# Weight chunks with seven block products: another order of sums, splits and settlements, and other places for the last chunk's slabs

## The chip, the cores and the metric

The kernel runs on one core of one Trainium2 chip. The metric is the device time in microseconds (us); three runs of the kernel before gave 1120.53, 1124.59 and 1125.94 us, median 1124.59.

## The reference, cut to what matters

Two decoder layers over 512 prompt tokens and 32 sample tokens (544 columns): a recurrent mixer in layer 0, windowed attention in layer 1, and behind each mixer the same MLP, which is what the change touches.

```python
D_MODEL = 1024
D_FF = 4 * D_MODEL

def squared_relu_mlp(x, w_up, w_down):
    return jnp.square(jax.nn.relu(x @ w_up)) @ w_down
...
        xp = layer_norm(ALPHA * xp + squared_relu_mlp(xp, mlp_w_up[i], mlp_w_down[i]), ln2_g[i], ln2_b[i])
```

All products are float32 in quality. The kernel splits each operand into a rounded high part and the rest, and multiplies high by high, high by rest and rest by high: three matmuls for one.

## The kernel before

The hidden width of 4096 is cut into 8 chunks of 512. Tokens are taken in two halves, of 256 and 288 columns. Chunk 0 and chunk 7 of a layer are computed plainly. Chunks 1 to 6 use seven block products for eight, both for the up product (x times w_up) and for the down product (hidden times w_down). Each chunk has an up half of seven products, which TensorE does in the order U11, UT1, UT2, U21, UT3, UT4, U22, and a down half, D11, DT1, DT2, D22, DT3, D21, DT4. Each product is 24 matmuls, of 256 columns in U11, U21, U22, D11, D22 and D21 and of 288 in the others, with two waits for banks, one ahead of each half of it. Chunks 2 to 5 are one rolled loop (Fori), so one order of instructions serves all of them.

The names without a T are blocks of the weights as they lie in memory. The names with a T are sums of blocks, and the DMA makes them: a block stands in one of four stage buffers, and POOL issues a DMA that adds another block onto it (L2055). So stage buffers are chains: U11 becomes UT1, then UT2, then UT4, and then the next chunk's U11 is loaded there. U22 becomes UT3, then D22 is loaded and becomes DT3. U21 and D21 take turns in the third. D11 becomes DT1, then DT2, then DT4 in the fourth. In chunk 1 alone, UT2 and UT4 stand in a buffer of their own, first_raw. A link of a chain can start only when the split of the one before it is done.

Splitting one weight (split_in) is an ACT copy that rounds into w_hi (L808) and a DVE subtraction into w_lo (L1315). TensorE waits for the second. ACT must also wait until the place in w_hi that it writes has been used up (PLACE, BEFORE, slot_free).

What ACT does between splits: keep (L1041) copies a finished up product from a bank so that the next product can add onto the bank. Product j has two tiles t, so keep(2, 0) takes the first tile of UT2, keep(4, 0) the first tile of UT3. UT2's tile t waits for keep(0, t), UT3's for keep(2, t), UT4's for keep(4, t). rectify, square_hi, square_raw and part_hi make from the kept sums the seven inputs of the down half, H11, H22, H12 and their sums S1 to S4. DVE adds banks onto kept products (combine, L1696), makes sums (part_sum, L1708) and the rest parts (part_lo, L1704), and settles each pair of down banks into acc (settle, L1719). In the order of the down products: D11 reads H11, DT1 S1, DT2 S2, D22 S4, DT3 S3, D21 H12, DT4 H22.

Every engine runs its own list in the order in which the code is written. So an instruction that waits holds up all that stands behind it on its engine, and the order by hand in chunk (one for each engine), load_around (SP, plain loads, L673) and all_sums (POOL, adding loads) is what the change rewrites. The tables ROUND_WEIGHT, REST_WEIGHT, SETTLE_ORDER, KEEP_ORDER and REST_ORDER repeat those orders so that waits get the right counts.

Chunk 7's four up slabs were ordinary jobs: load on SP behind all of chunk 6's loads, split by L802 on ACT and L1309 on DVE. group_by_half is TensorE's loop over them. In layer 0, POOL then issues the loads and copies of the attention caches (L2108 to L2112).

## Time and profile before

| | |
|---|---|
| median of three runs | 1124.59 us |
| profiled execution | 1123.91 us, of which the span of the program is 1121.7 us |
| TensorE busy | 1067.0 us, 95% |
| VectorE (DVE) busy | 845.0 us, 75% |
| ScalarE (ACT) busy | 665.9 us, 59% |
| GpSimd (POOL) busy | 226.4 us, 20% |
| mean granted TensorE clock | 0.97 of full |

The layer-0 MLP chunks 1 to 7 run from 220 to 530 us of the span, those of layer 1 from 770 to 1095 us. A chunk is about 43 to 52 us. Times in rows are from the start of the span. A row of the timeline gives the start, the duration, engine, line and operation, and in brackets how long the engine sat idle before it and who ended that.

### The profile page before, as it was taken

Reading aid. Unit: us, or ns where it says so; the run is one execution under the profiler, and the core shown is the slowest. Engines: PE = TensorE matmul, PEld = TensorE weight load, DVE = VectorE, ACT = ScalarE, POOL = GpSimd, SP = SyncE. Lnnn points to the kernel's source line nnn. Section 1 sums busy time; section 2 is a strip of 40 time slices with the busy share of each in tenths; the row PEclk is TensorE's granted clock in tenths of the full one; section 3 lists DMA queues with packets and bytes.
Section 4 is the critical chain, followed back from the end, with each engine's and each line's share of the span. In section 5 each row is a group of like instructions: output and inputs, shape, how many; then the busy total and the mean of one; then the engine's idle time right before and its main releaser. Section 6 shows DMA issues by size and latency. Waiting matters only on the chain.

```text
span 1121.7 us, 21627 instructions
## 1 busy us (share of the span) xinstructions
PE 1067.0 (95%) x8247; PEld 1040.7 (93%) x8247; DVE 845.0 (75%) x1289; ACT 665.9 (59%) x1159; POOL 226.4 (20%) x285
## 2 busy tenths in 40 slices
PE   8999999989999999899999999998999999998996
PEld 8999999989999899899999778998999899898995
DVE  6999898868778777586875664896868678585775
ACT  5999857554654636453667775665654636445343
POOL 1111042011111111111244463200111111111023
PEclk9999999989999999998999999999999999998998
DMA  7322406176787686773141220262787686866502
GB/s 241 114 86 94 132 18 190 39 151 141 163 200 150 137 180 137 184 203 123 28 124 44 76 58 20 76 151 59 167 189 150 134 183 151 175 143 132 150 1 80
DMA packets 54460, 139.54 MB, mean 124 GB/s; under 512 B 5632, under 2 KB 21440, under 8 KB 54368
## 3 DMA queue, kind: packets, MB, share of 16 engines
q0 software_dynamic: 14512, 53.60, 27.4%
q1 hardware_dynamic: 39584, 84.32, 22.8%
q8 instruction: 50, 0.82, 0.3%
q10 hardware_dynamic: 288, 0.59, 0.2%
q14 instruction: 26, 0.21, 0.1%
HBM read 135.95 MB, written 3.56 MB: 124 GB/s over the span
## 4 chain that ended last, share of the span: by engine, by line
PE 57%; DMA 17%; DVE 12%; issue 6%; ACT 6%; POOL 2%; DVEq 0%; SPq 0%; ACTq 0%; POOLq 0%
DMA stage<-w_up 10%; PE bank L2167 8%; PE bank L2168 7%; PE bank L2169 7%; DMA stage<-w_down 7%; DVE w_lo L1315 5%; PE bank L2422 3%; PE bank L2424 3%; PE bank L2423 3%; PE bank L2254 3%; PE bank L2443 3%; PE bank L2441 3%; PE bank L2442 3%; PE bank L2255 3%; PE bank L2256 3%
## 5 line engine op out<-in xcount | busy, mean ns | idle before, releaser
L808 ACT ACTIVATE w_hi<-stage 128x1024 fp32r<-128x1024 f32 x164 | 170.5, 1055 | 246.7 <-DMA stage<-w_up 117.1
L1315 DVE TENSOR_TENSOR w_lo<-stage,w_hi 128x1024 fp32r<-128x1024 f32 x164 | 194.8, 1219 | 78.0 <-ACT w_hi L808 77.8
L2441 PE MATMUL bank<-part_hi,w_hi 128*128 128x288 f32 (+1 forms) x672 | 194.9, 290 | 0.4 <-DVE part_lo L1704 0.3
L2443 PE MATMUL bank<-part_hi,w_lo 128*128 128x288 f32 (+1 forms) x672 | 194.8, 290 | 0.0
L2442 PE MATMUL bank<-part_lo,w_hi 128*128 128x288 f32 (+1 forms) x672 | 194.4, 289 | 0.0
L2167 PE MATMUL bank<-x_hi,w_hi 128*128 128x288 f32 (+1 forms) x496 | 145.2, 293 | 1.0 <-issue 1.0
L2168 PE MATMUL bank<-x_lo,w_hi 128*128 128x288 f32 (+1 forms) x496 | 143.7, 290 | 0.0
L2169 PE MATMUL bank<-x_hi,w_lo 128*128 128x288 f32 (+1 forms) x496 | 143.1, 288 | 0.0
L2441 PEld LDWEIGHTS bank<-part_hi,w_hi 128*128 128x128 f32 x672 | 127.2, 189 | 0.8 <-issue 0.5
L2442 PEld LDWEIGHTS bank<-part_lo,w_hi 128*128 128x128 f32 x672 | 127.5, 190 | 0.0
L2443 PEld LDWEIGHTS bank<-part_hi,w_lo 128*128 128x128 f32 x672 | 127.3, 189 | 0.0
L2422 PE MATMUL bank<-s_hi,w_hi 128*128 128x288 f32 (+1 forms) x384 | 114.5, 298 | 9.4 <-ACT h L1041 9.3
L1719 DVE TENSOR_TENSOR acc<-acc,bank 128x512 f32<-128x512 f32 (+1 forms) x168 | 113.0, 709 | 8.9 <-PE bank L2443 8.8
L2423 PE MATMUL bank<-s_lo,w_hi 128*128 128x288 f32 (+1 forms) x384 | 112.9, 294 | 0.0
L2424 PE MATMUL bank<-s_hi,w_lo 128*128 128x288 f32 (+1 forms) x384 | 112.7, 294 | 0.0
L2422 PE MATMUL bank<-x_hi,w_hi 128*128 128x256 f32 (+1 forms) x288 | 89.5, 311 | 22.8 <-ACT h L1041 19.0
L2055 POOL DMA_DIRECT2D stage<-w_down x48 | 41.4, 863 | 267.7 <-DVE w_lo L1315 267.7
L2167 PEld LDWEIGHTS bank<-x_hi,w_hi 128*128 128x128 f32 x496 | 93.2, 188 | 2.3 <-issue 2.1
L2169 PEld LDWEIGHTS bank<-x_hi,w_lo 128*128 128x128 f32 x496 | 93.4, 188 | 0.0
L2168 PEld LDWEIGHTS bank<-x_lo,w_hi 128*128 128x128 f32 x496 | 93.3, 188 | 0.0
L2055 POOL DMA_DIRECT2D stage<-w_up x44 | 41.7, 949 | 253.5 <-DVE w_lo L1315 231.6
L2254 PE MATMUL bank<-x_hi,w_hi 128*128 128x256 f32 (+1 forms) x288 | 85.0, 295 | 5.3 <-DVE acc L1719 5.3
(293 smaller groups left out, 2954.8 us busy)
## 6 DMA issues: line engine op xcount, KB each, us to landing
stage<-w_up SPq DMA_DIRECT2D x54, 512.0 KB, 3.9
stage<-w_down SPq DMA_DIRECT2D x52, 512.0 KB, 5.8
stage<-w_down POOLq DMA_DIRECT2D x48, 512.0 KB, 5.5
stage<-w_up POOLq DMA_DIRECT2D x44, 512.0 KB, 7.4
stage<-w_qkv SPq DMA_DIRECT2D x10, 512.0 KB, 4.3
stage<-w_x SPq DMA_DIRECT2D x8, 512.0 KB, 5.0
stage<-w_y SPq DMA_DIRECT2D x8, 512.0 KB, 3.4
stage<-w_out SPq DMA_DIRECT2D x8, 512.0 KB, 3.7
```

What stands on the lines that cost most here:

```text
L808: A(w_hi[:, slot_of(l, k), :], raw_of(l, c, k), ACT.Copy).then_inc(s_whi, 1)
L1315: vt.tensor_tensor(w_lo[:, s, :], raw_of(l, c, k), w_hi[:, s, :].bitcast(F32), ALU.subtract)\
L2167: mm(out, wh, xh, start=(k == 0), stop=False)
L2168: mm(out, wh, xl, start=False, stop=False)
L2169: ins = mm(out, wl, xh, start=False, stop=(k == last))
L2254: mm(out, wh, xh, start=(k == 0), stop=False)
L2422: mm(out, wh, xh[:, k, :], start=(fresh and k == 0), stop=False, skip_group_check=True)
L2423: mm(out, wh, xl[:, k, :], start=False, stop=False, skip_group_check=True)
L2424: ins = mm(out, wl, xh[:, k, :], start=False, stop=(k == 3), skip_group_check=True)
L2441: mm(out, wh, xh[:, k, :], start=(fresh and k == 0), stop=False, skip_group_check=True)
L2442: mm(out, wh, xl[:, k, :], start=False, stop=False, skip_group_check=True)
L2443: ins = mm(out, wl, xh[:, k, :], start=False, stop=(k == 1), skip_group_check=True)
```

## The change

The arithmetic stays the same: every product, split, sum and settlement of before is there once. What changes is the order and some places.

- POOL: the sum UT1 of the next chunk is issued ahead of DT4 instead of behind it, and UT2 and UT3 of the next chunk follow at the end of a chunk's list in place of the start of the next one's.
- SP: the next chunk's D11 is loaded at the end of a chunk's list, ahead of U21.
- ACT and DVE: another order of splits, keeps, squares, rest parts and settlements in a chunk. On ACT, D22's split now stands ahead of keep(4, 0), and square_hi and square_raw of H11 behind it; the splits DT3, D21 and the next UT1 stand ahead of part_hi of S4. On DVE, DT2's split stands ahead of the sum S2, and the next UT1's split ahead of D21's.
- Places in w_hi and w_lo are dealt out anew, so that the waits of slot_free follow.
- First chunk: U22 is split straight behind UT1, and UT2 behind the first accumulation, both ahead of the down sums of chunk 0; on ACT ahead of the second scaling of the residual.
- Last chunk: its four up slabs are loaded and split inside chunk 6, where the next chunk's U11, UT1, U22 and UT2 would be (bring_slab, slab_in).
- POOL's cache loads in layer 0 wait until the last down slab of chunk 7 is split.

The diff, cut to its core:

```diff
@@ -78,29 +78,30 @@
 H11, H22, S1, S2, H12, S4, S3, H21 = range(8)
 HIDDEN_WIDTH = {H11: 256, H12: 256, S4: 256, H22: HW, S1: HW, S2: HW, S3: HW}
 ROUND_ORDER = (H11, H22, S1, H12, S3, S2, S4)
-REST_ORDER = (H11, H22, S1, S2, H12, S4, S3)
+REST_ORDER = (H11, H22, S1, H12, S2, S4, S3)
...
-
-
-FIRST = (U11, UT1, UT2, U22)
-ROUND_WEIGHT = ((D11, 0), (U21, 0), (UT3, 0), (UT4, 0), (DT1, 0), (D22, 0), (U11, 1), (DT2, 0), (D21, 0), (DT3, 0),
-                (DT4, 0), (UT1, 1), (U22, 1), (UT2, 1))
-REST_WEIGHT = ((D11, 0), (U21, 0), (UT3, 0), (UT4, 0), (DT1, 0), (D22, 0), (U11, 1), (DT2, 0), (DT3, 0), (D21, 0),
-               (UT1, 1), (DT4, 0), (U22, 1), (UT2, 1))
+PLACE = {U11: 0, UT3: 0, UT1: 1, U22: 2, DT2: 2, UT2: 3, UT4: 3, DT3: 3, U21: 4, D22: 4,
+         D11: 5, D21: 5, DT1: 6, DT4: 6}
+BEFORE = {U11: (UT3, -1), UT3: (U11, 0), UT1: (UT1, -1), U22: (DT2, -1), DT2: (U22, 0), UT2: (DT3, -1), UT4: (UT2, 0),
+          DT3: (UT4, 0), U21: (D22, -1), D22: (U21, 0), D11: (D21, -1), D21: (D11, 0), DT1: (DT4, -1), DT4: (DT1, 0)}
+
+
+FIRST = (U11, UT1, U22, UT2)
+ROUND_WEIGHT = ((D11, 0), (U21, 0), (UT3, 0), (UT4, 0), (DT1, 0), (D22, 0), (U11, 1), (DT2, 0), (DT3, 0), (D21, 0),
+                (UT1, 1), (DT4, 0), (U22, 1), (UT2, 1))
+REST_WEIGHT = ((D11, 0), (U21, 0), (UT3, 0), (UT4, 0), (DT1, 0), (D22, 0), (U11, 1), (DT2, 0), (DT3, 0), (UT1, 1),
+               (D21, 0), (DT4, 0), (U22, 1), (UT2, 1))
 SPLITS = len(ROUND_WEIGHT)
-KEEP_ORDER = ((0, 0), (0, 1), (2, 1), (2, 0), (4, 0), (4, 1), (5, 1))
+SLAB_AFTER = (U11, UT1, U22, UT2)
+KEEP_ORDER = ((0, 0), (0, 1), (2, 0), (2, 1), (4, 0), (4, 1), (5, 1))
 COMBINE_ORDER = (U21, UT1, U22)
 RECTIFY_ORDER = (H11, H22, H12)
 SQUARE_ORDER = (H11, H22, H21, H12)
-SETTLE_ORDER = ((0, 0), (0, 1), (1, 0), (2, 0), (1, 1), (2, 1), (3, 0), (3, 1), (4, 0), (4, 1), (5, 0), (6, 0),
-                (6, 1), (5, 1))
+SETTLE_ORDER = ((0, 0), (0, 1), (1, 1), (1, 0), (2, 0), (2, 1), (3, 0), (3, 1), (4, 0), (4, 1), (5, 1), (5, 0),
+                (6, 0), (6, 1))
 SUM_ORDER = (S1, S3, S2, S4)
 
...
+            for n in (0, 0, 0, 1):
+                loads[(st0 + n) % STAGES] += 16
+                up_slab_at[l].append(((st0 + n) % STAGES, loads[(st0 + n) % STAGES]))
...
@@ -675,16 +688,29 @@
             def load_around(l, c, i=0):
 
                 last = c == CHUNKS - 2
-                if c > 1:
-                    bring(l, c, D11, s_xd, down_block(l, c, 0, 0, i), split_done(l, c - 1, DT4, i))
                 bring(l, c, D22, s_yin, down_block(l, c, 1, 1, i), split_done(l, c, UT3, i))
                 if not last:
                     bring(l, c + 1, U11, s_xu, up_block(l, c + 1, 0, 0, i), split_done(l, c, UT1 if c == 1 else UT4, i))
+                else:
+                    bring_slab(l, 0)
                 bring(l, c, D21, s_zin, down_block(l, c, 1, 0, i), split_done(l, c, U21, i))
                 if not last:
                     bring(l, c + 1, U22, s_yin, up_block(l, c + 1, 1, 1, i), split_done(l, c, DT3, i))
+                else:
+                    bring_slab(l, 1)
+                    bring_slab(l, 3)
+                    bring_slab(l, 2)
+                if not last:
+                    bring(l, c + 1, D11, s_xd, down_block(l, c + 1, 0, 0, i), split_done(l, c, DT4, i))
                 if not last:
                     bring(l, c + 1, U21, s_zin, up_block(l, c + 1, 1, 0, i), split_done(l, c, D21, i))
+
+            def bring_slab(l, k):
+
+                c = CHUNKS - 2
+                sp.wait_ge(*(split_done(l, c, UT4), split_done(l, c + 1, 0), split_done(l, c + 1, 1), split_done(l, c, DT3))[k])
+                st = up_slab_at[l][k][0]
+                sp.dma_start(stage[:, st, :], up_quad(l, c + 1, k)).then_inc(s_arrived[st], 16)
 
...
-                for k in range(4):
-                    load(j7 + k, up_quad(l, CHUNKS - 1, k))
...
+
+            def slab_in(l, k):
+
+                st, count = up_slab_at[l][k]
+                w = job_at[("chunk", l, CHUNKS - 1)][1] + k
+                act.wait_ge(s_arrived[st], count)
+                act.wait_ge(*free_at[w - SLOTS])
+                A(w_hi[:, w % SLOTS, :], stage[:, st, :], ACT.Copy).then_inc(s_whi, 1)
...
@@ -1069,51 +1101,59 @@
 
                 first, last = c == 1, c == CHUNKS - 2
                 h_low, h_mid, h_far = h11[:, :, 0:256], h12[:, :, :], h22[:, :, :]
+                keep(l, c, i, 0, 0, 4, h11[:, 0, 0:256])
                 split_in(l, c, D11, i)
-                keep(l, c, i, 0, 0, 4, h11[:, 0, 0:256])
                 split_in(l, c, U21, i)
+                if first:
+                    token_sum(l, 4, s4_hi[:, :, :], raw_b[:, :, 0:256])
                 split_in(l, c, UT3, i)
                 keep(l, c, i, 0, 1, 4, h11[:, 1, 0:256])
                 if first:
-                    token_sum(l, 4, s4_hi[:, :, :], raw_b[:, :, 0:256])
-                split_in(l, c, UT4, i)
-                keep(l, c, i, 2, 1, 4, h12[:, 1, :], -1.0)
-                if first:
                     act.wait_ge(s_slo, 4 * l + 3)
                     token_sum(l, 3, s3_hi[:, :, :], raw_a[:, :, :])
+                split_in(l, c, UT4, i)
                 keep(l, c, i, 2, 0, 4, h12[:, 0, :], -1.0)
+                keep(l, c, i, 2, 1, 4, h12[:, 1, :], -1.0)
                 split_in(l, c, DT1, i)
                 rectify(l, c, i, H11, h_low)
+                split_in(l, c, D22, i)
+                keep(l, c, i, 4, 0, 4, h22[:, 0, :], -1.0)
                 square_hi(l, H11, h_low)
-                square_raw(h_low)
-                keep(l, c, i, 4, 0, 4, h22[:, 0, :], -1.0)
-                split_in(l, c, D22, i)
                 keep(l, c, i, 4, 1, 4, h22[:, 1, :], -1.0)
                 if not last:
                     split_in(l, c + 1, U11, i)
+                else:
+                    slab_in(l, 0)
                 rectify(l, c, i, H22, h_far)
+                square_raw(h_low)
                 square_hi(l, H22, h_far)
                 keep_rectified(l, c, i)
                 square_raw(h_far)
                 act.wait_ge(*kept(l, c, 5, 1, i))
                 square_raw(h21[:, :, :])
+                part_hi(l, c, i, S1)
                 split_in(l, c, DT2, i)
-                part_hi(l, c, i, S1)
                 rectify(l, c, i, H12, h_mid)
                 square_hi(l, H12, h_mid)
                 part_hi(l, c, i, S3)
                 square_raw(h_mid)
                 part_hi(l, c, i, S2)
+                split_in(l, c, DT3, i)
                 split_in(l, c, D21, i)
+                if not last:
+                    split_in(l, c + 1, UT1, i)
+                else:
+                    slab_in(l, 1)
                 part_hi(l, c, i, S4)
-                split_in(l, c, DT3, i)
                 split_in(l, c, DT4, i)
                 if not last:
-                    split_in(l, c + 1, UT1, i)
-                if not last:
                     split_in(l, c + 1, U22, i)
+                else:
+                    slab_in(l, 2)
                 if not last:
                     split_in(l, c + 1, UT2, i)
+                else:
+                    slab_in(l, 3)
 
...
-                for k in FIRST[:2]:
+                for k in FIRST:
                     split_in(l, 1, k)
                 scale_residual(l, 1)
-                for k in FIRST[2:]:
-                    split_in(l, 1, k)
                 chunk(l, 1)
                 with act.Fori(0, CHUNKS - 4) as i:
                     chunk(l, 2, i)
                 chunk(l, CHUNKS - 2)
-                split(range(j7, j7 + 4))
                 for q in range(4):
                     for k in ((0, 1), (2,), (3,), ())[q]:
                         split([j7 + 4 + k])
...
@@ -1719,10 +1763,12 @@
                 vt.tensor_tensor(a, a, bank[:, b0:b0 + 2, 0:n], ALU.subtract if j in (2, 4) else ALU.add)\
                     .then_inc(s_acc, 1)
 
-            def chunk(l, c, i=0, slabs=lambda k: None):
+            def chunk(l, c, i=0):
 
                 first, last = c == 1, c == CHUNKS - 2
                 split_in(l, c, D11, i)
+                if first:
+                    token_lo(l, 3, s4_lo[:, :, :], s4_hi[:, :, :], raw_b[:, :, 0:256])
                 split_in(l, c, U21, i)
                 split_in(l, c, UT3, i)
                 if first:
@@ -1730,11 +1776,13 @@
                 split_in(l, c, UT4, i)
                 combine(l, c, i, U21, 0, h11[:, :, 0:256], (0, 1))
                 split_in(l, c, DT1, i)
-                part_lo(l, c, i, H11)
                 combine(l, c, i, UT1, 6, h22[:, :, :], (4, 1))
                 split_in(l, c, D22, i)
                 if not last:
                     split_in(l, c + 1, U11, i)
+                else:
+                    slab_in(l, 0)
+                part_lo(l, c, i, H11)
                 part_lo(l, c, i, H22)
                 dve.wait_ge(*squared(l, c, H21, i))
                 dve.wait_ge(*squared(l, c, H22, i))
@@ -1744,43 +1792,45 @@
                 dve.wait_ge(*squared(l, c, H11, i))
                 part_sum(h21[:, :, :], h11[:, :, :], h21[:, :, :], ALU.subtract)
                 part_lo(l, c, i, S1)
-                settle(l, c, i, 0, 0)
+                split_in(l, c, DT2, i)
                 dve.wait_ge(*summed(l, c, S1, i))
                 dve.wait_ge(*squared(l, c, H11, i))
                 part_sum(h22[:, :, :], h22[:, :, :], h11[:, :, :], ALU.subtract)
-                split_in(l, c, DT2, i)
+                settle(l, c, i, 0, 0)
+                part_lo(l, c, i, H12)
                 part_lo(l, c, i, S2)
-                part_lo(l, c, i, H12)
+                settle(l, c, i, 0, 1)
                 dve.wait_ge(*summed(l, c, S2, i))
                 part_sum(h12[:, :, :], h12[:, :, :], h22[:, :, 0:256], ALU.add)
-                settle(l, c, i, 0, 1)
+                settle(l, c, i, 1, 1)
                 settle(l, c, i, 1, 0)
                 part_lo(l, c, i, S4)
+                part_lo(l, c, i, S3)
+                split_in(l, c, DT3, i)
                 settle(l, c, i, 2, 0)
-                settle(l, c, i, 1, 1)
-                split_in(l, c, DT3, i)
-                part_lo(l, c, i, S3)
+                if not last:
+                    split_in(l, c + 1, UT1, i)
+                else:
+                    slab_in(l, 1)
                 settle(l, c, i, 2, 1)
+                split_in(l, c, D21, i)
                 settle(l, c, i, 3, 0)
                 settle(l, c, i, 3, 1)
-                split_in(l, c, D21, i)
-                if not last:
-                    split_in(l, c + 1, UT1, i)
                 split_in(l, c, DT4, i)
                 settle(l, c, i, 4, 0)
                 settle(l, c, i, 4, 1)
-                slabs(0)
                 if not last:
                     split_in(l, c + 1, U22, i)
-                slabs(1)
+                else:
+                    slab_in(l, 2)
+                settle(l, c, i, 5, 1)
                 settle(l, c, i, 5, 0)
                 settle(l, c, i, 6, 0)
-                settle(l, c, i, 6, 1)
-                slabs(2)
-                settle(l, c, i, 5, 1)
                 if not last:
                     split_in(l, c + 1, UT2, i)
-                slabs(3)
+                else:
+                    slab_in(l, 3)
+                settle(l, c, i, 6, 1)
 
...
                 accumulate_pair(l, 1, 0)
+                split_in(l, 1, UT2)
                 accumulate_pair(l, 1, 2)
                 accumulate_pair(l, 1, 4)
                 accumulate(l, 6)
                 accumulate(l, 7)
-                split_in(l, 1, UT2)
-                split_in(l, 1, U22)
                 token_sum_4(l)
-                token_lo(l, 3, s4_lo[:, :, :], s4_hi[:, :, :], raw_b[:, :, 0:256])
                 chunk(l, 1)
                 with dve.Fori(0, CHUNKS - 4) as i:
                     chunk(l, 2, i)
-                chunk(l, CHUNKS - 2, slabs=lambda k: split([j7 + k]))
+                chunk(l, CHUNKS - 2)
                 for q in range(4):
...
+                up_sum(l, 1, UT3, 0, 1, s_uy, split_done(l, 1, U22))
                 for c in range(1, CHUNKS - 1):
-                    if c > 1:
-                        up_sum(l, c, UT2, 1, 1, s_ux, split_done(l, c, UT1))
-                    up_sum(l, c, UT3, 0, 1, s_uy, split_done(l, c, U22))
                     up_sum(l, c, UT4, 1, 0, s_first if c == 1 else s_ux, split_done(l, c, UT2))
                     down_sum(l, c, DT1, 0, 1, s_dx, split_done(l, c, D11))
                     down_sum(l, c, DT2, 1, 1, s_dx, split_done(l, c, DT1))
                     down_sum(l, c, DT3, 0, 1, s_dy, split_done(l, c, D22))
+                    if c < CHUNKS - 2:
+                        up_sum(l, c + 1, UT1, 0, 1, s_ux, split_done(l, c + 1, U11))
                     down_sum(l, c, DT4, 1, 0, s_dx, split_done(l, c, DT2))
                     if c < CHUNKS - 2:
-                        up_sum(l, c + 1, UT1, 0, 1, s_ux, split_done(l, c + 1, U11))
+                        up_sum(l, c + 1, UT2, 1, 1, s_ux, split_done(l, c + 1, UT1))
+                    if c < CHUNKS - 2:
+                        up_sum(l, c + 1, UT3, 0, 1, s_uy, split_done(l, c + 1, U22))
...
+            pool.wait_ge(s_wlo, slabs_of(0, CHUNKS - 1) + 8)
             pool.wait_ge(*up_done(0, CHUNKS - 2, 6, 1))
```

## Rows read from the trace of the kernel before

**Rows 1.** The page's second part: TensorE's granted clock in 40 slices of the span.
```profile
PEclk9999999989999999998999999999999999998998
```

**Rows 2.** Waits of PE: engine, line, waited for: total us, times, longest.
```profile
PE bank L2422 <- ACT h L1041: 28.4, 19, 3.6
PE bank L2254 <- DVE acc L1719: 5.3, 3, 2.0
```

**Rows 3.** Stretches: length, busy us (x) of PE PEld DVE ACT POOL, PEclk, DMA.
```profile
220.11:222.93 2.82, 2.82 (x26) 2.82 (x25) 2.62 (x3) 2.27 (x3) 0.00 (x0) 1.00 0.00 0
317.34:338.82 21.48, 21.48 (x170) 21.37 (x169) 13.41 (x14) 14.38 (x22) 3.46 (x4) 1.00 0.89 200
432.59:453.97 21.38, 21.38 (x170) 21.38 (x169) 20.36 (x28) 9.39 (x13) 3.49 (x4) 1.00 0.59 130
453.97:480.25 26.28, 23.30 (x170) 22.92 (x169) 12.96 (x14) 14.36 (x22) 3.46 (x4) 0.94 0.79 174
220.11:271.75 51.64, 47.05 (x338) 46.46 (x337) 39.43 (x46) 26.30 (x36) 7.82 (x9) 0.90 0.64 135
271.75:501.60 229.85, 219.27 (x1682) 216.99 (x1680) 169.46 (x207) 122.66 (x175) 35.24 (x42) 0.99 0.74 168
501.60:519.25 17.65, 14.18 (x98) 13.81 (x97) 10.98 (x15) 8.07 (x12) 0.00 (x0) 0.81 0.53 172
769.66:819.37 49.71, 45.26 (x338) 44.64 (x337) 39.51 (x46) 26.07 (x36) 7.79 (x9) 0.93 0.65 142
819.37:1054.23 234.86, 221.91 (x1682) 219.71 (x1681) 171.44 (x209) 124.09 (x176) 31.95 (x37) 0.97 0.71 156
1054.23:1069.29 15.06, 13.19 (x99) 12.98 (x98) 9.00 (x12) 6.52 (x11) 0.00 (x0) 0.89 0.36 110
```

**Rows 4.** The chain that ended last, layer 0, end of chunk 5 and chunk 6.
```profile
448.65 8.27 DMA stage<-w_up
...
459.56 0.87 POOL stage L2055
...
460.69 8.69 DMA stage<-w_down
...
469.40 1.06 ACT w_hi L808
...
472.60 0.37 PE bank L2422
```

**Rows 5.** Timeline of POOL, the adding loads of chunk 5's down half (DT3, DT4, UT1).
```profile
428.33 0.87 POOL L2055 DMA_DIRECT2D stage<-w_down  x1 [3.04 <-DVE w_lo L1315]
...
438.14 1.22 POOL L2055 DMA_DIRECT2D stage<-w_up  x1
```

**Rows 6.** Timeline of DVE, chunk 5: splits of D22 and the next U11.
```profile
426.82 2.35 DVE L1315 TENSOR_TENSOR w_lo<-stage,w_hi 128x1024 fp32r<-128x1024 f32 x2
```

**Rows 7.** DMA issues in 444 to 453: size, us from issue to landing.
```profile
stage<-w_up SPq DMA_DIRECT2D x2, 512.0 KB, 3.7
...
stage<-w_down SPq DMA_DIRECT2D x1, 512.0 KB, 7.6
```

**Rows 8.** Timelines, chunk 1 of layer 0: U22's split (DVE), UT3's split (ACT), UT2's second tile (PE).
```profile
221.81 1.22 DVE L1315 TENSOR_TENSOR w_lo<-stage,w_hi 128x1024 fp32r<-128x1024 f32 x1
...
229.53 1.06 ACT L808 ACTIVATE w_hi<-stage 128x1024 fp32r<-128x1024 f32 x1 [6.48 <-DMA stage<-w_up]
...
230.92 0.40 PE L2422 MATMUL bank<-s_hi,w_hi 128*128 128x288 f32 x1 [3.02 <-ACT h L1041]
```

**Rows 9.** Timelines, chunk 7 of layer 0: the second slab's split (ACT), the first square (POOL).
```profile
500.19 1.06 ACT L802 ACTIVATE w_hi<-stage 128x1024 fp32r<-128x1024 f32 x1 [5.55 <-DMA stage<-w_up]
...
525.04 0.40 POOL L2030 COPY sumsq_a<-sqt 128x256 f32<-128x256 f32 x1 [35.91 <-ACT sqt L950]
```

**Rows 10.** Timeline of SP, chunk 6: D22's load; DMA issues then: its us to landing.
```profile
462.69 0.34 SPq L673 DMA_DIRECT2D stage<-w_down  x1
...
stage<-w_down SPq DMA_DIRECT2D x1, 512.0 KB, 6.9
```

40 lines of the change are left out of this document (25 added, 15 removed).

## The prediction

> **What bounds the kernel now.** I read the page's clock line first, then the waits of TensorE, then the stretches of the two MLPs, then one chain of waits and the timelines around it. TensorE is busy 95% of the span, so only its gaps and its slow stretches can be won. The clock line is under 9 in a few slices [rows 1], and nearly all the waiting of PE is at three lines of the MLP: 28.4 us of waits at L2422 for a kept product, 5.3 at the last chunk's first group L2254 for a settlement [rows 2].
>
> To size this I take a chunk that does not wait. The reader should see in [rows 3] an up half of 21.48 us (chunk 3 of layer 0) and a down half of 21.38 (chunk 5), both with PE busy throughout at clock 1.00, the 2.4 GHz level. Together 42.86 us is a clean chunk. Against that stand six stretches. Chunk 1 took 51.64 and 49.71 us: 8.78 and 6.85 too long. Chunks 2 to 6 took 229.85 and 234.86, less 5 x 42.86 = 214.3: 15.5 and 20.6 too long. Chunk 7's first group is 96 matmuls of 256 columns; 24 of them took 2.82 us in the first product, so 11.28, and the stretches are 17.65 and 15.06: 6.4 and 3.8 too long. Sum: 15.6 + 36.1 + 10.2 = 61.9 us in both layers. Part of it is idle time and part is what follows it: those stretches show a clock of 0.81 to 0.99, that is, pieces at 1.2 GHz after a gap [rows 3]. A program with no gap left in the MLPs would take 1123.9 - 61.9 = 1062 us; that is the floor.
>
> The worst up half of layer 0 is chunk 6: 26.28 us against 21.48, of which 2.98 idle and the rest at the lower clock [rows 3]. The chain that ended last shows why [rows 4]. UT2's sum is issued at 448.65 and takes 8.27; its split releases UT4's sum at 459.56; DT1's sum goes out at 460.69 and takes 8.69; then ACT rounds DT1 at 469.40, does H11's rectify and two squares, and only then the keep that UT4's matmuls at 472.60 wait for. So TensorE waits for a copy of its own bank, held up in ACT's list behind a split that waits for a DMA.
>
> **The change part by part.** All times are of layer 0, chunks 5 and 6; the down half of chunk 5 starts at 432.59, chunk 6 at 453.97 [rows 3].
>
> *The sums' order on POOL.* The next UT1's sum went out at 438.14, behind DT4's, though U11's split ended at 429.17 (426.82 + 2.35) [rows 5, 6]. Now it follows DT3's, issued at 428.33, so near 429.5. With the 8.7 of the slowest sum in [rows 4] it lands by 438.2. Its DVE split now stands behind S3's and S4's rest parts, DT3's split and one settlement; counted with 0.6 to 1.2 an item that is about 445.0. UT2's sum then goes out at 445.2, not 448.65, and lands by 453.5 (8.27), ahead of chunk 6. Its rest is ready near 455.5, and UT4's sum goes at 455.7, not 459.56.
>
> *D11 and DT1.* D11 is loaded on DT4's split, as before, near 449.5. That load took 7.6 beside UT2's sum; loads without one took 3.7 [rows 7]. Now it lands at 453.2 to 457.1. ACT splits it behind keep(0, 0), from 455.9, so DT1's sum goes out between 458.3 and 460.7. I take 458.3, because UT2's sum is then out of the way. DT1's sum took 8.69 beside UT4, D22 and D21 [rows 4]; UT4's is now over earlier, and I take 7.5, with 8.69 as the upper bound and UT3's 6.5 in chunk 1 (223.03 to 229.53 [rows 8]) as the lower. It lands at 465.8. Behind it: its split 1.06, rectify 0.6, D22's split 1.0, keep 0.35, and some 0.2 of signals, 3.2 in all, 469.0. Without a gap UT4's product is due at 453.97 + 2 x 2.82 + 3 x 3.25 = 469.4, where 3.25 is (21.48 - 3 x 2.82) / 4. So there is 0.4 us left with these values; with 8.69 UT4 waits 0.8, with nothing gained on D11 it waits 3.2 as now. I take 0.5 us a chunk, since one up half of before did close with no gap at all [rows 3]. Ten chunks: 5 us of the 36.1 stay.
>
> *The down half's order.* DVE is busy 20.36 of 21.38 us there [rows 3]: its list is the second bound. The same instructions stay in it, so their sum costs nothing; their order can. DT2's split moves ahead of the sum S2, and H12's rest ahead of S2's. S2's rest then ends near 438.6 and DT2's product is due at 432.59 + 2.82 + 3.25 = 438.66. On ACT, S4's rounding stands behind three splits, 437.4 + 3 x 1.0 + 0.6 = 441.0, its rest ends at 441.8, and D22's product is due at 441.9. These fit by a tenth. From below nothing can be won, as the half has no gap; from above 0.6 us each half. I take 0.3 for twelve halves: 3.6 us new.
>
> *First chunk.* UT2's second tile waited 3.02 for keep(0, 1), which stands behind UT3's split at 229.53, and UT3's sum had waited for U22's split that ended at 223.03 [rows 8]. Now U22 is split right behind UT1, near 215.5, so the sum lands 6.5 later at 222.0; ACT, with D11, U21, S4's token sum and UT3 in line from 221.9, comes to keep(0, 1) near 226.5, and the tile is due at 227.8. The accumulations on DVE come 2.3 us later. They are covered: DVE stood idle between them, and their banks are first needed by UT1 and U21. The same shift brings UT4, DT1 and D22 forward. D22's load waits for UT3's rest and stands ahead of keep(4, 0) now; bounds 0 to 3 us, I take 1.0 a layer, nearer the small stalls of the later chunks. So 13.6 of the 15.6 go.
>
> *Last chunk.* ACT sat idle 5.55 us until the second slab's load landed at 500.19 [rows 9], with chunk 7 due at 501.6, and settlements on DVE stood behind slabs. Now each slab takes the turn of a weight whose link was a sum; a plain load in the same place is shorter (3.7 against 8.27), so slabs are never later than those weights. The settlement that the group's first tiles need stands ahead of the last slab. I leave 0.5 a layer; 9.2 of 10.2 go. The caches' loads on POOL are held until the last down slab is split, in front of the squares: five issues at 0.5 to 1 us. POOL was idle for 35.91 us before its first square at 525.04 [rows 9], so I count 0; if the slabs' splits end after 522, up to 2 us.
>
> *Clock.* The halves with no gap ran at 1.00, chunk 6's up half, with 2.98 us idle, at 0.94 [rows 3]. It lost 4.80 in all, so its piece at 1.2 GHz cost 1.8. I leave one such piece.
>
> Sum: 5 + 3.6 + 2 + 1 + 1.8 = 13.4 us stay of 61.9, gain 48.5, and 1123.9 - 48.5 = 1075.4 us. The profiled execution stands 0.7 us below the median of the runs, so 1076.
>
> *A rule against it.* The DMA traffic of a chunk is unchanged, and the chunk gets shorter. The clean up half already ran with a DMA share of 0.89 [rows 3]. The Trainium skill, page "DMA: Bandwidth & Descriptors", section "Issuing engines are not separate DMA queues", says that DMAs "will ultimately run on the same 16 DMA engines and interleave with each other". The D11 load at 7.6 beside a sum, and 3.7 without, agrees. By that rule a sum moved forward lengthens what it now meets, and the sums would keep their 8 us; this is the first rival.
>
> **The rivals.** *First, traffic moves the bound to D22.* D22's load is issued when UT3's rest is ready, and UT3's sum still waits for U22's split, which nothing in the change brings forward. If D22's load goes out at 462.7 and takes 6.9 as before [rows 10], it lands at 469.6, D22's split ends at 470.7 and keep(4, 0), now behind it, at 471.0: UT4 waits 1.6. For: D22's split stood behind the keep before, and DMA share. Against: D21's load and UT4's sum overlap it less now. Price: 16 us left in place of 5, no long gap and so no more of the lower clock: 1076 + 11 = 1087.
>
> *Second, the UT1 sum is not forwarded,* because POOL's list is held at DT3 by D22's late split, or ACT reaches UT1 late. The steady chunks keep two thirds of their 36.1, first and last chunk gain their 22.8: 1124.6 - 22.8 - 12 + 3.6 + 1.8 = 1095; with nothing from the steady chunks 1105.
>
> *Third, slower than before: the down half waits for the UT1 sum.* It stands on ACT ahead of S4's rounding, which must be done by 441.3, so UT1's split must begin by 439.6. The sum leaves at 429.5; at over 10 us it makes TensorE wait, 1 us for 1 us, in ten chunks, and the clock falls at long gaps. To eat 48.5 us and go 0.5% past it takes some 5.5 us a chunk, a sum of 15.5 us, 1130 us in all. Against: none in [rows 4] took over 8.7. For: it would meet DT3's and DT2's sums in one queue.
>
> **How the numbers follow.** Forecast 0.61 (1064 to 1083), first rival 0.22 (1083 to 1093), second 0.08 (1093 to 1115), third 0.05, and 0.04 that losses elsewhere leave it within 0.5%, about what a measurement of this kernel can tell from no change. So faster 0.91, same 0.04, slower 0.05. The range runs from 1064, just above the floor of 1062, to 1096, with the first rival and the better part of the second; outside are 0.03 below and some 0.14 above.
>
> **What would show it.** In the profile after: UT1's sum about 1.1 us behind DT3's and ahead of DT4's; DT1's sum at most 5 us into a chunk; up halves of 21.5 to 22 us and the clock at 1.00 over chunks 2 to 6; the waits of L2422 for L1041 under 8 us in total; down halves of 21.4 to 21.7, with any wait there at part_lo or settle; chunk 1 under 44; the last group near 11.5. The prediction is wrong if D22's split is what keep(4, 0) stands behind for longest, if the waits of PE name the down half's L2441, or if loads and sums both get longer than now.

## The result

The kernel after took 1062.76 us (median of four runs, 1062.08 to 1063.49) beside 1122.86 us for the kernel before: ratio 0.9463, 95% interval 0.9435 to 0.9491. The forecast was 1076 with a range from 1064 to 1096, so the time came out 1.2 us below the range's low end. The direction held; the size did not, and the experiments show that one step behind it did not hold either.

The profiled execution took 1063.49 us, its span 1061.3, 60.4 less than before. The page of the kernel after, its head and its clock line, which answers to [rows 1]:

```profile
span 1061.3 us, 21612 instructions
...
PE 1045.2 (98%) x8247; PEld 1022.6 (96%) x8247; DVE 840.5 (79%) x1289; ACT 662.7 (62%) x1159; POOL 226.3 (21%) x285
...
PEclk9999999999999999999999999999999999999998
```

TensorE is busy for 98% of the span, and in its clock line only the last slice is below 9. The waits of PE in the kernel after (line, waited for: total us, times, longest):

```profile
PE bank L2289 <- DVE w_lo L1346: 2.8, 2, 2.1
PE bank L2745 <- DVE diag L2026: 1.4, 1, 1.4
PE bank L2330 <- DVE ones L1413: 1.1, 1, 1.1
```

None of these lines is in an MLP chunk. The two of [rows 2], 28.4 us for kept products and 5.3 for settlements, are gone. The stretches of the kernel after, columns as in [rows 3]: chunk 5's up half and down half, then for each layer chunk 1, chunks 2 to 6 and chunk 7's first group:

```profile
391.62:413.09 21.47, 21.47 (x170) 21.35 (x169) 12.79 (x14) 13.35 (x21) 4.32 (x5) 1.00 0.85 178
413.09:434.73 21.64, 21.64 (x171) 21.42 (x170) 21.36 (x30) 11.12 (x14) 2.59 (x3) 1.00 0.76 162
...
219.58:262.29 42.71, 42.71 (x339) 42.71 (x338) 38.03 (x46) 26.69 (x37) 6.03 (x7) 1.00 0.76 163
262.29:477.43 215.14, 215.14 (x1682) 213.77 (x1681) 170.73 (x211) 124.05 (x177) 31.95 (x37) 1.00 0.79 172
477.43:488.85 11.42, 11.42 (x98) 11.42 (x97) 6.95 (x10) 4.56 (x9) 0.00 (x0) 1.00 0.52 173
739.33:782.03 42.70, 42.70 (x338) 42.70 (x337) 38.01 (x46) 26.69 (x37) 6.04 (x7) 1.00 0.74 163
782.03:997.17 215.14, 215.12 (x1682) 213.73 (x1681) 170.68 (x211) 124.52 (x177) 31.83 (x37) 1.00 0.79 172
997.17:1008.59 11.42, 11.42 (x98) 11.42 (x97) 6.88 (x10) 4.07 (x9) 0.00 (x0) 1.00 0.22 76
```

In every row the busy time of PE equals the length (within 0.02 us), at clock 1.00. Against [rows 3], chunk 1 is 8.93 and 7.01 us shorter, chunks 2 to 6 are 14.71 and 19.72, the last group 6.23 and 3.64. Together that is 60.24 of the 60.4 us. So the whole gain lies where the prediction put the excess of 61.9 us; of that, 1.7 us is left.

### The profile page after: what moved, and what is told of

Its sections match the earlier page's. It is cut to its first block, busy times and chain, and to the rows that moved or that the text cites. A ratio compares the mean times of both kernels' runs of the same rounds, so it can differ in the third digit from the quotient of the medians.

```text
span 1061.3 us, 21612 instructions
## 1 busy us (share of the span) xinstructions
PE 1045.2 (98%) x8247; PEld 1022.6 (96%) x8247; DVE 840.5 (79%) x1289; ACT 662.7 (62%) x1159; POOL 226.3 (21%) x285
## 4 chain that ended last, share of the span: by engine, by line
PE 92%; DVE 2%; ACT 2%; issue 1%; POOL 1%; DMA 1%; SPq 0%; DVEq 0%; POOLq 0%; ACTq 0%
PE bank L2493 8%; PE bank L2474 8%; PE bank L2495 8%; PE bank L2219 8%; PE bank L2494 8%; PE bank L2475 8%; PE bank L2476 8%; PE bank L2220 8%; PE bank L2221 8%; PE bank L2306 3%; PE bank L2307 3%; PE bank L2308 3%; PE bank L2614 1%; PE bank L2588 1%; PE bank L2447 1%
## 5 line engine op out<-in xcount | busy, mean ns | idle before, releaser
L832 ACT ACTIVATE w_hi<-stage 128x1024 fp32r<-128x1024 f32 x164 | 168.3, 1053 | 128.9 <-DMA stage<-w_up 74.1
L1352 DVE TENSOR_TENSOR w_lo<-stage,w_hi 128x1024 fp32r<-128x1024 f32 x164 | 197.0, 1219 | 57.8 <-ACT w_hi L832 57.7
L2104 POOL DMA_DIRECT2D stage<-w_up x44 | 38.1, 867 | 220.4 <-DVE w_lo L1352 198.9
L2474 PE MATMUL bank<-x_hi,w_hi 128*128 128x256 f32 (+1 forms) x288 | 83.1, 289 | 0.0
L2306 PE MATMUL bank<-x_hi,w_hi 128*128 128x256 f32 (+1 forms) x288 | 82.8, 288 | 0.0
```

What stands on the lines that cost most here:

```text
L832: A(w_hi[:, slot_of(l, k), :], raw_of(l, c, k), ACT.Copy).then_inc(s_whi, 1)
L1352: vt.tensor_tensor(w_lo[:, s, :], raw_of(l, c, k), w_hi[:, s, :].bitcast(F32), ALU.subtract)\
L2306: mm(out, wh, xh, start=(k == 0), stop=False)
L2474: mm(out, wh, xh[:, k, :], start=(fresh and k == 0), stop=False, skip_group_check=True)
```

## The experiments

In the profiles of this section, "UT2's sum takes" and times "ahead of" or "into" a chunk are medians over chunks 3 to 6 of both layers, read from the DMA issues and set against the chunk's first matmul. A half runs from its first matmul to that of the next half; that of chunk 6 ends at chunk 7's first matmul, so a wait there is counted in it. Nothing of the reference is left out in any of these kernels. The kernel before had medians from 1111.8 to 1122.9 us in the six groups of runs that were timed together, while four kernels close to the one after (e6, e12, e14, e20) stayed within 1061.8 to 1064.2; so sizes of a few us are read from the stretches, and ratios stand for the rest.

### Chunks 2 to 6: the order of the sums

**The POOL order taken back in the kernel after.**

```diff
                     down_sum(l, c, DT3, 0, 1, s_dy, split_done(l, c, D22))
+                    down_sum(l, c, DT4, 1, 0, s_dx, split_done(l, c, DT2))
                     if c < CHUNKS - 2:
                         up_sum(l, c + 1, UT1, 0, 1, s_ux, split_done(l, c + 1, U11))
-                    down_sum(l, c, DT4, 1, 0, s_dx, split_done(l, c, DT2))
```

> The changed kernel with one thing put back: on POOL the next UT1's sum stands behind DT4's again. ACT and DVE keep the new order, in which UT1's split stands ahead of S4's rounding. Theory A (the sums' times on the DMA carry the gain, and a late sum holds up the engines' lists): UT1's sum lands 11 us into the down half in place of 5, S4's rounding comes 4 to 5 us late, TensorE waits about 4.5 us in the down half of chunks 1 to 5 of both layers, ten times, and loses 1.8 us more to the lower clock after such a gap: 1063 + 45 to 63 = 1108 to 1126 us, with the waits at the down product D22 on part_lo. Theory B (the gain comes from the order on ACT and DVE; when the sum goes out is indifferent): 1063 to 1066 us.

Measured: 1135.78 us, ratio 1.0152 (1.0064 to 1.0240) to before: 0.6 to 2.4% slower than the kernel that the change started from. The waits of PE in this kernel, then one of them in the timelines of POOL, ACT and PE, and the stretch of its down half:

```profile
PE bank L2493 <- DVE part_lo L1748: 39.2, 8, 5.4
PE bank L2493 <- issue: 9.9, 2, 4.9
```

```profile
445.41 0.87 POOL L2104 DMA_DIRECT2D stage<-w_down  x1 [6.07 <-DVE w_lo L1352]
445.94 1.22 POOL L2104 DMA_DIRECT2D stage<-w_up  x1
...
453.99 1.06 ACT L832 ACTIVATE w_hi<-stage 128x1024 fp32r<-128x1024 f32 x1 [5.59 <-DMA stage<-w_up]
454.95 0.61 ACT L1098 ACTIVATE part_hi<-h 128x512 fp32r<-128x512 f32 x1
...
456.52 0.58 PE L2493 MATMUL bank<-part_hi,w_hi 128*128 128x256 f32 x1 [5.21 <-DVE part_lo L1748]
```

```profile
441.66:471.45 29.79, 24.59 (x171) 24.14 (x170) 21.86 (x30) 11.12 (x14) 3.48 (x4) 0.89 0.60 127
```

UT1's sum goes out 4.3 us into the down half, behind DT4's. ACT waits 5.59 us for it, S4's rounding stands behind it in the list, and TensorE waits 5.21. All ten down halves that have a next UT1 wait like this, and the clock over this stretch is 0.89. In the kernel after that sum leaves at 411.04, 2.05 us ahead of the down half; so here it comes 6.3 us later, takes 8.0 and not about 7, and TensorE waits 5.2 of those 7.3: the link had 2 us to spare. The third rival's mechanism is real, at the price that the prediction gave it. It let UT1's split begin 7.0 us into the down half at the latest (439.6 less 432.59); here the sum lands 12.2 us in, and the wait is the difference.

**The same POOL order, alone, in the kernel before.** The edit is the one above, the other way round.

> The kernel before with one thing of the change: on POOL the next UT1's sum ahead of DT4's. UT1's rounding on ACT and its rest on DVE stay behind DT4's. Theory A: UT1's sum lands 9 us earlier, but its split keeps its place in the lists, so UT2's sum still leaves 5.3 us ahead of the next chunk, and the waits at UT3 and UT4 stay: 1117 to 1124 us. A reader who takes the forwarded sum itself for the cause (theory C) expects most of the 36 us of the steady chunks: 1085 to 1095 us.

Measured: 1124.25 us, ratio 1.0044 (0.9999 to 1.0089). In this kernel PE waits as in [rows 2], `L2422 <- ACT h L1041: 30.2` us in 23 waits. Its timeline of POOL:

```profile
431.54 0.86 POOL L2055 DMA_DIRECT2D stage<-w_up  x1 [0.27 <-DVE w_lo L1315]
438.18 0.86 POOL L2055 DMA_DIRECT2D stage<-w_down  x1 [5.77 <-DVE w_lo L1315]
449.23 0.87 POOL L2055 DMA_DIRECT2D stage<-w_up  x1 [10.19 <-DVE w_lo L1315]
```

UT1's sum leaves 7 to 9 us earlier, and UT2's, in the last row, still 5.3 us ahead of the chunk (which starts at 454.55), where it left before. The split between them had kept its place behind DT4's.

**Sum, split and places together in the kernel before.** Beside the POOL order of the kernel after, its PLACE and BEFORE, and UT1's split moved on both engines. The cut shows ACT; on DVE it stands ahead of settle(2, 1), and D21's split moves ahead of settle(3, 0), too:

```diff
                 split_in(l, c, D21, i)
+                if not last:
+                    split_in(l, c + 1, UT1, i)
                 part_hi(l, c, i, S4)
```

> The kernel before with one chain of the change: the new places in w_hi and w_lo, POOL's new order of sums, and the next UT1's split forward on both engines (ACT ahead of S4's rounding, DVE ahead of D21's split). Keeps, squares, first chunk, last chunk, caches and D11's load stay as before. Theory A (UT1's sum and its split together, so that UT2's sum leaves 3 us earlier and does not meet D11's load): the up halves of chunks 2 to 6 fall from 24 to 28 us to about 21.5, so some 34 of the 36 us of these chunks go: 1084 to 1092 us, the first chunk's and the last group's losses stay. Theory D (it takes more than this chain, the keeps' new order among it): up halves of 23 us or more, 1100 us or more.

Measured: 1090.18 us, ratio 0.9727 (0.9655 to 0.9799). To chunk 7's first matmul, chunks 2 to 6 take 217.5 and 217.4 us. The first of these ends in a wait of 1.8 us for a settlement, which [rows 3] counts with chunk 7; without it 31.6 of the 36.1 us of excess go. UT2's sum leaves 8.3 us ahead of the chunk and takes 5.7; nine of the ten up halves take 21.4 to 21.9 us, one takes 23.1. One such up half of this kernel:

```profile
357.42:378.83 21.41, 21.41 (x170) 21.35 (x169) 14.26 (x15) 13.62 (x21) 4.32 (x5) 1.00 0.83 179
```

**Only the split put late again in the kernel after** (ACT: UT1 behind DT4; DVE: UT1 behind settle(3, 1)).

> The changed kernel with the next UT1's split late again: on ACT behind DT4's, on DVE behind the settlements of D22 and ahead of DT4's. The sum itself stays forward. UT2's sum then leaves near 6 us ahead of the chunk in place of 8.7, and meets D11's and U21's loads. Theory A in its strong form (that meeting is what cost before): UT2's sum takes 7 to 8 us, DT1 lands 2 us later and TensorE waits 0 to 1 us a chunk: 1064 to 1075 us. If the rest of the new order leaves enough room: within 1 us of 1063.

Measured: 1066.07 us, ratio 0.9520 (0.9451 to 0.9589). The up halves of chunks 2 to 6 stay clean, at most 21.48 us but for one of 21.85. What is lost lies at the last chunk, where the second slab takes UT1's turn: chunk 6's down halves of 22.64 and 23.02, not 21.38, with waits of 1.1 and 1.5 us for a settlement ahead of chunk 7. This was a surprise. UT2's sum leaves 5.7 us ahead of the chunk, as late as in e2, yet it takes 6.0 us where it takes 8.25 there. So its moment of issue was not what decided, and the next six kernels look for what did.

### Chunks 2 to 6: the order of two loads

**D11's load ahead of U21's, beside the POOL order, in the kernel before.**

```diff
-                if c > 1:
-                    bring(l, c, D11, s_xd, down_block(l, c, 0, 0, i), split_done(l, c - 1, DT4, i))
...
                 if not last:
+                    bring(l, c + 1, D11, s_xd, down_block(l, c + 1, 0, 0, i), split_done(l, c, DT4, i))
+                if not last:
                     bring(l, c + 1, U21, s_zin, up_block(l, c + 1, 1, 0, i), split_done(l, c, D21, i))
```

> The kernel before with two moves: the next UT1's sum ahead of DT4's on POOL (as in e2_before_pool_only) and the next chunk's D11 loaded at the end of a chunk's list on SP, ahead of U21. Question: UT2's sum leaves 5.3 us ahead of the chunk in e2_before_pool_only and takes 8.25 (median of eight), and it leaves 5.7 ahead in e5_ut1_split_late and takes 6.0, whose up halves are clean. Which difference between the two makes it short? Loads theory: the order of the D11 and U21 loads on SP. Then UT2's sum takes about 6 here, UT4's sum leaves 3 us into the chunk, the up halves of chunks 2 to 6 are 21.5 to 22 and the time falls by some 28 us, ratio 0.975. Places theory: the places in w_hi. Then it stays at 8.2, the up halves at 24 to 26, ratio 1.00.

Measured: 1087.39 us, ratio 0.9699 (0.9641 to 0.9757). UT2's sum leaves 5.3 ahead, as in e2, and takes 6.0; UT4's goes out 3.4 us into the chunk and not 5.6.

**The places alone, beside the POOL order.**

> The kernel before with the next UT1's sum ahead of DT4's on POOL and the places of the kernel after (PLACE, BEFORE), the orders of SP, ACT and DVE untouched. In e2_before_pool_only ACT waits for a bank until 12.4 us into the down half, since DT4 is written to D22's place, and UT1's split stands behind it. Places theory: with DT4 in DT1's place this wait goes, UT1's split and UT2's sum come at least 0.5 us earlier, the sums at the border of the chunks get shorter, up halves 21.5 to 22.5, ratio 0.975 to 0.98. Loads theory: UT2's sum stays above 8 us, DT1's sum lands 14 to 15 us into the chunk, ratio 0.995 to 1.00.

Measured: 1126.27 us, ratio 1.0063 (1.0023 to 1.0104). ACT starts UT1's split 1.6 us earlier, its DVE part ends where it ended (5.6 ahead of the chunk), UT2's sum takes 8.3. The places gain nothing by themselves.

**Both.**

> The kernel before with UT1's sum forward on POOL, the new places and D11's load ahead of U21's; the orders of ACT and DVE stay those of before. If either loads or places are the cause, it is as fast as the faster of e15_d11_load_first and e16_places, ratio about 0.975. If both are needed, it alone is fast. If it is at 1.00 too, the cause lies in the orders of ACT and DVE, and the first rival to that is DT3's split ahead of S4's rounding.

Measured: 1088.96 us, ratio 0.9713 (0.9655 to 0.9771), as with the load order.

**The late split with the old order of the two loads, in the kernel after.** The edit swaps the last two loads of SP's list.

> e5_ut1_split_late (the kernel after with the next UT1's split at its late place) with the two last loads of SP's list swapped: U21 ahead of D11, as before the change. Loads theory: UT2's sum goes from 6.0 back to about 8.2, UT4's sum leaves 5.5 us into the chunk and not 2.9, DT1's sum lands near 14, the up halves of chunks 2 to 6 are 23 to 26 and the time rises to 1085 to 1100 us. Places theory, or another cause in the orders of ACT and DVE: UT2's sum stays at 6, up halves 21.5, 1066 us.

Measured: 1066.64 us, ratio 0.9511 (0.9454 to 0.9569): a miss for the loads theory as it was put. UT2's sum stays at 6.0. But D21's split ends earlier in this kernel, so U21's load leaves 8.2 us ahead of the chunk, 2.45 ahead of the sum, and has landed (it took 3.8) 1.3 us behind the sum's issue. The single chunks run from 5.8 to 6.2; chunk 2 of layer 0, outside the median, has 7.4 and an up half of 22.35. What counts is not which load comes first in the list but how late U21's runs into the sum: for 1.3 us here, for 2.3 in the kernel before.

**The load order alone in the kernel before.** The edit is that of e15 without the POOL order.

> The kernel before with one move: the next chunk's D11 is loaded at the end of a chunk's list on SP, ahead of U21. No sum, split, place or slab moves. In e15_d11_load_first and e18_places_and_d11, U21's load leaves 1.46 us behind UT2's sum and the sum takes 6.0; in the kernel before, e2_before_pool_only and e16_places it leaves 1.26 ahead and the sum takes 8.3. Theory: U21's load running into UT2's sum is the whole cause, and UT1's sum forward is not needed, since UT2's sum leaves 5.3 ahead of the chunk with and without it. Then this kernel is as fast as e15_d11_load_first: UT2's sum 6.0, UT4's sum 3.4 into the chunk, up halves 21.4 to 22.1, ratio 0.970, some 1087 us. Rival: both moves are needed, because the UT1 sum at its old place lands late and its split then holds UT2's sum in some chunks. Then up halves stay at 22.5 to 26 and the ratio is above 0.98.

Measured: 1088.98 us, ratio 0.9747 (0.9691 to 0.9803). The kernel's stretch of chunks 2 to 6 in layer 0, for the 229.85 of [rows 3], and its wait for the kept products, for the 28.4 of [rows 2]:

```profile
271.89:491.46 219.57, 215.40 (x1682) 213.78 (x1681) 172.08 (x209) 125.48 (x176) 35.17 (x42) 1.00 0.78 180
```

```profile
PE bank L2422 <- ACT h L1041: 8.3, 9, 3.1
```

In layer 1 the chunks take 215.9 (before 234.86). The stretch of layer 0 ends in a wait of 1.6 us for a settlement, which [rows 3] counts with chunk 7. So one load moved gives 30.8 of the 36.1 us, with UT1's sum at its old place; the up halves take 21.4 to 22.5. The rows that show why are the DMA issues (us from issue to landing at the end) and issue times around the sum. In the kernel before, ahead of chunk 6, U21's load left near 447.4, UT2's sum at 448.65 and D11's load at 449.52; U21's load and the sum:

```profile
stage<-w_up SPq DMA_DIRECT2D x1, 512.0 KB, 3.5
stage<-w_up POOLq DMA_DIRECT2D x1, 512.0 KB, 8.3
```

The same kernel ahead of chunk 3: the timelines of SP (U21's load, D11's) and of POOL (UT2's sum), then the sum among the DMA issues:

```profile
310.44 0.33 SPq L673 DMA_DIRECT2D stage<-w_up  x1
313.53 0.34 SPq L673 DMA_DIRECT2D stage<-w_down  x1
...
312.48 0.87 POOL L2055 DMA_DIRECT2D stage<-w_up  x1 [10.07 <-DVE w_lo L1315]
```

```profile
stage<-w_up POOLq DMA_DIRECT2D x1, 512.0 KB, 5.7
```

And in e19, ahead of chunk 6: the timeline of SP (D11's load, then U21's), then the DMA issues of the sum, which POOL issued at 441.67, and of those two loads:

```profile
442.54 0.33 SPq L673 DMA_DIRECT2D stage<-w_down  x1
443.14 0.33 SPq L673 DMA_DIRECT2D stage<-w_up  x1
```

```profile
stage<-w_up POOLq DMA_DIRECT2D x1, 512.0 KB, 5.9
stage<-w_down SPq DMA_DIRECT2D x1, 512.0 KB, 5.9
stage<-w_up SPq DMA_DIRECT2D x1, 512.0 KB, 7.1
```

In eight of the ten chunks 2 to 6 of before, U21's load leaves 1.3 us ahead of UT2's sum and is in the queues for 2.3 us of it; D11's follows 1 us behind, and the sum takes 7.9 to 8.6. Chunk 3 of layer 0 is an experiment that the kernel before made by itself: there the load leaves 2.04 ahead, the sum takes 5.7, and that is the clean up half of 21.48 us in [rows 3]. In e19 the load goes last and is itself the slow one, 7.1 us, which nobody waits for. The Trainium skill, page "DMA: Bandwidth & Descriptors", section "Issuing engines are not separate DMA queues", says that transfers of all issuers run on the same 16 engines and interleave; these rows agree, and show that the order and spacing of the issues choose which of them pays. Not every chunk fits: in chunk 2 of layer 1 of before the load left 1.4 ahead and the sum took 6.6.

**The same two loads swapped back in the kernel after.**

> The kernel after with the last two loads of SP's list swapped back: U21's ahead of D11's. U21's load should then leave near 8.2 us ahead of the chunk, 0.5 behind UT2's sum at 8.7 ahead, and D11's stays at 4.9 ahead. Theory (U21's load beside UT2's sum lengthens it): the sum goes from 5.6 to 6 to 8 us, but it lands by 0.7 ahead of the chunk at worst, where the sums at 5.3 ahead landed 3 us behind the start, so UT4's and DT1's sums hardly move and no gap opens: up halves 21.5, 1063 to 1066 us. Rival: the load order is what the kernel after depends on, too: up halves of 22.5 and more, above 1075 us.

Measured: 1062.18 us, ratio 0.9519 (0.9468 to 0.9571). U21's load leaves 1.6 us behind UT2's sum, and both take 5.6 and 5.5 us. Its chunks 2 to 6:

```profile
260.70:475.80 215.10, 215.10 (x1683) 213.74 (x1682) 170.66 (x211) 124.28 (x177) 31.97 (x37) 1.00 0.79 172
```

So the kernel after has two remedies for the same loss, the sum early and the load late. With one undone (e20, e5) the other carries the chunk. With both undone (e17) D21's split, 1.7 us earlier than in the kernel before, still keeps the load clear of most of the sum; no run takes that away, too.

**More traffic in the kernel after.** SP issues one more transfer of 512 KB in each of the chunks 1 to 6, right behind D22's load (twelve in all, 6.3 MB, into the output's memory, which is written over later).

> The changed kernel with one more transfer of 512 KB in each of the chunks 1 to 6, a copy from w_up in HBM to the output's memory (overwritten at the end), issued by SP right behind D22's load, so beside DT1's and UT4's sums. Theory A (there is room for it as long as DT1 lands by 12 us into a chunk and D22 by 13.8): D22's load lengthens from 4.8 to some 7 us, DT1's sum from 5.6 to some 7, TensorE waits 0 to 1 us in a chunk: 1062 to 1073 us. The rule that all DMAs share the engines, taken as the bound (share 0.8 to 0.9 in the up halves): every transfer lengthens, the waits return at UT3 and UT4 with 2 to 3 us a chunk: 1085 to 1100 us.

Measured: 1064.16 us, ratio 0.9500 (0.9431 to 0.9568), no new wait over 0.3 us in the chunks:

```profile
262.00:476.00 214.00, 213.85 (x1672) 212.47 (x1671) 169.46 (x210) 123.45 (x177) 31.94 (x37) 1.00 0.83 184
```

The DMA share rises from 0.79 to 0.83 and nothing moves. The amount of traffic was not the bound, against the first rival. The extra transfers leave some 7 us into the chunk, beside D22's load, and not beside UT2's sum; what cost the kernel before was the company that this one sum met.

### First chunk

**U22's and UT2's splits put back** behind the accumulations (DVE) and the second scale_residual (ACT).

> The changed kernel with the first chunk's part put back: U22 and UT2 are split behind the five accumulations of chunk 0's down product (DVE), and behind the second scaling of the residual (ACT). Theory A: UT3's sum leaves 6 us later, keep(0, 1) behind its split comes 2 to 3 us late, and what follows in chunk 1 too, with a stretch at 1.2 GHz: 5 to 8 us a layer, 1073 to 1079 us, and chunks 2 to 6 stay clean. If the first chunk's new order matters only through POOL's and DVE's other changes: 1063 to 1066 us.

Measured: 1067.05 us, ratio 0.9530 (0.9450 to 0.9610). Chunk 1's up halves take 22.93 and 22.62 us, not 21.33: 2.9 us in both layers, with one wait of 1.0 for a keep in each.

**Also the token sums put back** (ACT: token_sum 4 behind UT3's split, 3 behind UT4's; DVE: token_lo ahead of the chunk).

> The changed kernel with all of the first chunk's part put back: U22 and UT2 split behind the accumulations, and the token sums 4 and 3 in their old places (ACT rounds sum 4 behind UT3's split and keep(0, 1); DVE makes its rest ahead of D11's split, so that D11's, U21's and UT3's splits stand behind it). With the first alone chunk 1's up half was 22.9 and 22.6 us. Theory A: the second gap of before, U21 waiting for its rest behind the token sum's, returns, and with it a stretch at 1.2 GHz: up half of chunk 1 at 27 to 29 us, 1071 to 1078 us. If the token sums' place is indifferent: 1063 to 1067 us.

Measured: 1077.11 us, ratio 0.9618 (0.9549 to 0.9687). Up halves 29.59 and 27.38, as in the kernel before (30.26 and 28.33). The waits of PE in this kernel:

```profile
PE bank L2475 <- DVE w_lo L1354: 5.2, 2, 2.6
PE bank L2475 <- ACT h L1073: 4.5, 3, 1.8
```

Of chunk 1's 14.3 us in both layers, the splits put back alone cost 2.9 (e4), and the places of two token sums cost 11.4 on top of them. That does not make 11.4 the worth of the token sums' places by themselves, since no run puts them back with the splits early, and the timelines of ACT and DVE in this kernel tie the two together:

```profile
226.16 1.06 ACT L832 ACTIVATE w_hi<-stage 128x1024 fp32r<-128x1024 f32 x1 [4.04 <-DMA stage<-w_up]
227.12 0.36 ACT L1073 ACTIVATE h<-bank 128x256 f32<-128x256 f32 x1
227.38 1.05 ACT L1068 ACTIVATE s_hi<-raw_b 128x1024 fp32r<-128x1024 f32 x1
...
228.47 1.23 DVE L1402 TENSOR_TENSOR s_lo<-raw_b,s_hi 128x1024 fp32r<-128x1024 f32 x1 [4.92 <-ACT s_hi L1068]
```

UT3's split on ACT waits 4.04 us for its sum, which could leave only behind U22's late split; keep(0, 1) and the rounding of token sum 4 stand behind it. On DVE the rest of that token sum waits 4.92 us for the rounding, with the splits of D11 and U21 behind it. So the first gap of TensorE, 1.5 us, is for keep(0, 1) behind UT3's split, and the second, 2.6, for U21's rest behind the token sum's; the third, 1.8, is for keep(4, 0), which stands behind the splits of DT1 and D22. They follow each other within 14 us in layer 0, and a piece at 1.2 GHz comes behind the last.

### Last chunk

**The wait ahead of the caches' loads taken out of the kernel after.**

```diff
-            pool.wait_ge(s_wlo, slabs_of(0, CHUNKS - 1) + 8)
```

> The changed kernel without POOL's wait ahead of the caches' loads, so that they are issued at the end of chunk 6 of layer 0 as before. The slabs are in by then and the down slabs are not due for 10 us. Theory A: no gap comes back in chunk 7, 1062 to 1064.5 us. If the caches' loads were what cost layer 0's last group 2.6 us more than layer 1's (17.65 against 15.06): the group goes from 11.4 to 13 or 14 us, 1065 to 1067 us.

Measured: 1066.08 us, ratio 0.9609 (0.9561 to 0.9657). Chunk 6's down half in layer 0 takes 23.54 to chunk 7's first matmul, not 21.38, with one wait of 2.0 us for a settlement: the wait on POOL is worth 2.2 us. The prediction had nothing for it; the expectation's second case had the time, but looked for it in the last group. The slab loads issued in 462 to 480, in this kernel and then in the kernel after, and this kernel's split of the second slab on DVE:

```profile
stage<-w_up SPq DMA_DIRECT2D x2, 512.0 KB, 7.5
...
stage<-w_up SPq DMA_DIRECT2D x2, 512.0 KB, 4.0
...
477.52 1.23 DVE L1359 TENSOR_TENSOR w_lo<-stage,w_hi 128x1024 fp32r<-128x1024 f32 x1 [3.01 <-ACT w_hi L840]
```

Beside the caches' loads, issued from 461 on, the first two slabs take 7.5 us and not 4.0, and the settlements stand behind their splits on DVE.

**That wait, and settle(5, 1) ahead of slabs(2), in the kernel before;** its slabs keep their places.

> The kernel before with two small parts: the caches' loads held back, and the settlements (5, 0), (5, 1), (6, 0), (6, 1) all ahead of the third slab's split on DVE. The slabs stay where they were. If the last group's losses (6.4 and 3.8 us) came from the settlement behind the slab and the loads beside: they fall to 0 to 2 us each, 1112 to 1116 us against 1120 to 1123, and moving the slabs was not needed for them. If they came from the slabs' late loads: 1119 to 1123 us.

Measured: 1105.39 us, ratio 0.9948 (0.9916 to 0.9981). Both last groups take 11.42 us, so all that they had lost (6.4 and 3.8) is gone without any new place for a slab. Layer 1 has no caches' loads, so its 3.8 are the settlement's alone; how the 6.4 divide is open. The medians differ by 6.4 us and not by 10.2, but the runs of the kernel before in this group alone spread from 1101.5 to 1118.9. The up halves of chunks 2 to 6 stay at 23.2 to 28.0.

### Small orders on ACT and DVE

**keep(4, 0) ahead of D22's split again, behind both squares** (ACT, kernel after).

> The changed kernel with keep(4, 0) on ACT behind both squares of H11 and ahead of D22's split again, as before. Theory A: DT1 now lands 10.1 us into a chunk and UT4's product is due at 15.3; DT1's split, rectify, two squares and the keep take 3.2, so 13.3 is early enough and nothing changes: 1062 to 1064.5 us. Theory B (the squares' and D22's new place did it): a wait of 1 to 2 us at UT4 in each of ten chunks returns: 1073 to 1083 us.

Measured: 1061.84 us, ratio 0.9489 (0.9409 to 0.9570), up halves 21.38 to 21.41. The place of D22's split, which the first rival turned on, makes no difference once DT1's sum is early.

**S2's rest ahead of H12's again** (DVE, kernel after).

> The changed kernel with the rest part of S2 ahead of that of H12 on DVE, as before. In the changed kernel the down halves of chunks 2 to 5 are 21.62 to 21.66 us where those of chunks 1 and 6 are 21.38: DT2's product starts 0.15 us late, behind S2's rest. If S2's place is the cause, eight or ten halves shorten by 0.1 to 0.25 us: 1 to 2.5 us less than the changed kernel, 1060.5 to 1062 us. If the cause is something else in the loop: no change.

Measured: 1065.59 us, ratio 0.9606 (0.9571 to 0.9641). Down halves 21.83 in the loop and 21.57 in chunks 1 and 6, 0.2 more than after, with 0.2 us of waits in each loop half for S4's rest. This missed the expectation: the new order is the better one, by 2.4 us in all twelve halves.

**Both.**

> The changed kernel with S2's rest first and with keep(4, 0) behind H11's squares and ahead of D22's split (the old order of both). The second alone took 1061.84 us, with up halves of 21.41. If both small effects add: 1 to 2.5 us less than the changed kernel, and the shortest of all.

Measured: 1064.13 us, ratio 0.9600 (0.9565 to 0.9635): e7's down halves and e6's up halves. The 0.25 us by which the loop's down halves (21.63) exceed those of before (21.38) stay open: no wait over 0.15 us shows in them, and neither order removes it. Of it, 0.08 comes with the new places alone (21.46 in e16 and e18).

No kernel here is measurably faster than the one after.

## Why the prediction was right, and where it was wrong

The direction and the place of the gain were right. The step that failed is the sum of what stays, 13.4 us, and under it the durations of two sums, which the working took from a kernel in which each ran beside other transfers.

**The floor held.** 1123.9 less 61.9 is 1062, and the kernel after took 1062.8. The clean chunk of 42.86 us, taken from two halves that never wait, was found again as 42.71 and 43.1.

**The sum of what stays was too large,** 13.4 us against 1.7. Term by term, forecast and measured: the up halves of chunks 2 to 6, 5 and 0; twelve down halves, 3.6 and 2.0 (eight of them 0.25 longer, four not); the first chunk, 2 and 0; the last, 1 and 0.3 (11.42 twice for 11.28); the piece at 1.2 GHz, 1.8 and 0. The up halves of chunks 1 and 6, at 21.33, are 0.15 us shorter than the clean one, which takes 0.6 off again. Each term was put on links for which the working had found a slack: 0.4 us at UT4, a tenth at D22. A wait is what a link is late by, or nothing; half a microsecond on each is no bound. The range then left out its own floor.

**UT1's sum and the early sums** were placed well: UT1's leaves 1.14 us behind DT3's (forecast 1.1), UT4's 0.84 into the chunk (1.7), DT1's 4.5 into it (4.3). The timeline of POOL in the kernel after, DT3's sum, UT1's, DT4's and UT2's for [rows 5]:

```profile
409.90 0.86 POOL L2104 DMA_DIRECT2D stage<-w_down  x1 [2.95 <-DVE w_lo L1352]
411.04 0.86 POOL L2104 DMA_DIRECT2D stage<-w_up  x1 [0.27 <-DVE w_lo L1352]
416.84 0.87 POOL L2104 DMA_DIRECT2D stage<-w_down  x1 [4.94 <-DVE w_lo L1352]
426.04 0.86 POOL L2104 DMA_DIRECT2D stage<-w_up  x1 [8.34 <-DVE w_lo L1352]
```

**The lengths failed.** The working took UT2's sum at 8.27 us and DT1's at 7.5. They took 5.6 and 5.6; D22's load took 4.9 where 6.9 was taken, D11's 3.7 where 3.7 to 7.6 was. DT1 then lands at 10.1 and not at 11.8, and the 0.4 us of slack was 2.1. The prediction had the fact in hand, a load of 7.6 beside a sum and 3.7 without [rows 7], and used it only one way: what slows a load slows the sum too. One of its two loads of 3.7 was U21's, which did have UT2's sum beside it, for its last 2.3 us. It kept its time because it had gone first; the sum behind it paid.

**The cause in the steady chunks was incomplete.** The prediction held that UT1's sum behind DT4's was why UT2's was late and the chunk long. UT1's sum forward alone gains nothing (e2), with its split forward and UT2's sum early it does (e13), and so does a step that the prediction costed at nothing, D11's load ahead of U21's, with the sums untouched (e19). "D11 is loaded on DT4's split, as before" is true, but what moved was U21's load, from 1.3 us ahead of UT2's sum to 4.4 behind it. The chain in [rows 4] showed the 8.27 us; the step that failed was to take this duration as the sum's own.

**First chunk:** right in size, 15.9 us gained for 13.6 forecast. The reason given, U22's late split, is a real one, but with the token sums at their new places it is worth only 2.9 (e4). The working left out the second gap of chunk 1, which the waits of PE in the kernel before list on a line of their own:

```profile
PE bank L2422 <- DVE w_lo L1315: 3.8, 2, 2.3
```

The prediction speaks of three lines and shows two; this is the third, U21's rest, and it needs the token sums' places as well (e11). That the size came out so near is in part luck.

**Last chunk:** 9.9 gained, 9.2 forecast. The slabs' turns were not needed for it (e10), so the right size has a wrong reason in part; settle(5, 1) and POOL's wait are enough. The step that counted POOL's wait at 0 failed: it did not ask what the caches' loads meet on the DMA, only what stands behind them on POOL, and the wait is worth 2.2 (e8).

**Rivals.** The first fell: no wait behind D22's split, and more traffic does no harm (e12, e6). The second did not come about. The third did not either, but e1 shows its place and price, and that this change with one of its parts left out is slower than none.

## What to carry to other kernels

When a chain of waits runs through a transfer, compare its duration with the shortest of its size, and look which transfers are in flight beside it, above all which left just ahead of it: moving a load that nobody waits for can shorten one that everybody waits for. An early link gains only if the split behind it moves too, and a split moved ahead of its transfer holds up all of its engine's list. Where the working finds slack, leave nothing for that link, and let the range reach the floor.

## What the runs showed of the hardware

- Of the weights' transfers of 512 KB in the MLPs, an adding one took 5.2 to 5.8 us where nothing else was in flight (24 cases in all kernels) and up to 10.0 (e2) beside others; a plain load took 3.2 to 3.7 alone (66 cases) and up to 10.5 (e16).
- When a load left 1.3 us ahead of UT2's sum and another 1 us behind it, the sum took about 8.3 us (before, e2, e16), and the load ahead kept its 3.6. With the load ahead moved away from it, 2.0 ahead (one chunk of before) it took 5.7, 2.45 ahead (e17) 6.0, and 1.5 behind (e15, e19) 6.0. Single chunks stray from this by 1 to 1.7 us, and why is open.
- 6.3 MB of further transfers, issued beside D22's load, cost nothing that shows, at a DMA share of 0.83 (e12). Five loads of the caches beside two slab loads took these from 4.0 to 7.5 us (e8).
- Single gaps of 1.5 us (e5) and 2.0 us (e8) left the clock at 1.00; waits of 5.2 us (e1) and several gaps close together (e11) had a piece at 1.2 GHz behind them. Two near cases in layer 1 of the kernel before differ: waits of 0.3 and 1.96 us in chunk 4's up half left the clock at 1.00, and 0.6 and 1.98 in chunk 5's left it at 0.93 over the half.
- The kernel before varied between groups of runs by 1%, 1111.8 to 1122.9 us. The kernels with no gap over 0.3 us in the MLPs varied by 0.4% (1061.8 to 1065.6).
